# Four small TensorE items queued at other places of a two-block transformer kernel

## The reference

```
h = rmsnorm(x, g_mix);  z = h @ w_in
cb, cc, cv, q, k, v, f_logit, gate_c, gate_a = split(z)
log_f = log_sigmoid(f_logit + b_f)                 # one column per head, 8 heads
c = cumsum(log_f over the tokens)
logits = q k^T / sqrt(128) + c[query] - c[key], causal; attn = softmax(logits) v
conv_y = cb * causal_dwconv(cc * cv)
x = x + (sigmoid(..) * (conv_y @ w_conv_out) + sigmoid(..) * (attn @ w_attn_out)) @ w_mix_out
x = x + square(relu(rmsnorm(x, g_mlp) @ w_ff1)) @ w_ff2
x = rmsnorm(x, g_final)
```

## Time and profile before

| | |
|---|---|
| median of three runs | 2388.35 us |
| the three runs | 2388.16, 2388.35, 2389.65 us |
| profiled execution | 2390.3 us, of which the span of its instructions is 2388.2 us |
| PE busy | 2378.5 us of the span (100% in the page's rounding) |
| PEld, DVE, ACT busy | 2035.8, 1700.8, 1216.2 us |
| weights and the rest moved | 452.14 MB, mean 189 GB/s |

### The profile page before, as it was taken

One profiled execution on the slowest core, in us unless ns is written; L12 is line 12 of the kernel. 1 busy time (PEld: TensorE's weight loads), 2 busy tenths in 40 slices (PEclk: granted clock), 3 DMA queues, 4 the chain that ended last, 5 costly groups with the idle time before them and its releaser, 6 DMA issues.

```text
span 2388.2 us, 30674 instructions
## 1 busy us (share of the span) xinstructions
PE 2378.5 (100%) x12581; PEld 2035.8 (85%) x12581; DVE 1700.8 (71%) x1804; ACT 1216.2 (51%) x1427; POOL 0.2 (0%) x4
## 2 busy tenths in 40 slices
PE   9999999999999999999999999999999999999999
PEld 8788888888888888888888888888888888888887
DVE  5565666666567868868868667855788777886788
ACT  5354454555544545445445555555555455545554
POOL 0000000000000000000000000000000000000000
PEclk9999999999999999999999999999999999999999
DMA  7557566665565675656665565555655665566655
GB/s 252 160 162 204 161 196 192 192 188 197 189 185 172 216 223 183 218 175 203 200 192 188 183 185 168 168 177 185 186 181 193 199 193 177 183 217 189 187 171 181
DMA packets 238040, 452.14 MB, mean 189 GB/s; under 512 B 16570, under 2 KB 20780, under 8 KB 237772
## 3 DMA queue, kind: packets, MB, share of 16 engines
q1 hardware_dynamic: 237147, 449.07, 59.4%
q10 hardware_dynamic: 752, 1.12, 0.1%
HBM read 446.46 MB, written 3.67 MB: 188 GB/s over the span
## 4 chain that ended last, share of the span: by engine, by line
PE 96%; DVE 3%; ACT 1%; DMA 0%; issue 0%; SPq 0%; DVEq 0%; ACTq 0%
PE PS L72 96%; DVE WL L72 1%; ACT WH L72 1%; DVE PB L72 0%; DVE PT L72 0%; DVE XT L72 0%; DMA RAW<-in_w_in 0%; DVE TB L72 0%; DVE TA L72 0%; ACT TA L72 0%; ACT SQ L72 0%; DVE XHL L72 0%; ACT TB L72 0%; DVE TC L72 0%; DVE SEL L72 0%
## 5 line engine op out<-in xcount | busy, mean ns | idle before, releaser
L72 DVE TENSOR_TENSOR WL<-RAW,WH 128x1024 fp32r<-128x1024 f32 (+1 forms) x844 | 1001.8, 1204 | 517.0 <-ACT WH L72 514.9
L72 PE MATMUL PS<-XHL,WH 128*128 128x512 f32 x3984 | 1254.1, 396 | 2.2 <-DVE CR L72 1.3
L72 ACT ACTIVATE WH<-RAW 128x1024 fp32r<-128x1024 f32 (+1 forms) x845 | 867.1, 1041 | 735.7 <-PE PS L72 721.4
L72 PEld LDWEIGHTS PS<-XHL,WL 128*128 128x128 f32 x3968 | 746.1, 188 | 176.3
L72 PE MATMUL PS<-XHL,WL 128*128 128x256 f32 x3968 | 780.3, 278 | 0.0
L72 PE MATMUL PS<-WH,MHL 128*128 128x512 f32 x2000 | 624.6, 390 | 0.0
L72 PEld LDWEIGHTS PS<-XHL,WH 128*128 128x128 f32 x3984 | 607.2, 188 | 6.5 <-DVE CR L72 1.5
L72 PEld LDWEIGHTS PS<-WH,MHL 128*128 128x128 f32 x2000 | 375.5, 188 | 78.3 <-DVE XHL L72 0.4
L72 PE MATMUL PS<-WL,MHL 128*128 128x512 f32 x1000 | 389.1, 389 | 0.0
L72 PEld LDWEIGHTS PS<-WL,MHL 128*128 128x128 f32 x1000 | 187.8, 188 | 37.9
L72 ACT ACTIVATE MHL<-TA 128x1024 fp32r<-128x1024 f32 x33 | 35.0, 1061 | 121.9 <-DVE TA L72 121.9
(11 more groups left out here) (150 smaller groups left out, 1211.2 us busy)
## 6 DMA issues: line engine op xcount, KB each, us to landing
RAW<-in_w_ff SPq DMA_DIRECT2D x256, 512.0 KB, 4.1
RAW<-in_w_in SPq DMA_DIRECT2D x224, 512.0 KB, 3.9
RAW<-in_w_up SPq DMA_DIRECT2D x176, 512.0 KB, 4.1
RAW<-in_w_down SPq DMA_DIRECT2D x88, 512.0 KB, 4.4
RAW<-in_w_mix_out SPq DMA_DIRECT2D x32, 512.0 KB, 3.9
RAW<-in_w_out SPq DMA_DIRECT2D x32, 512.0 KB, 3.7
RAW<-in_w_conv_out SPq DMA_DIRECT2D x16, 512.0 KB, 3.7
RAW<-in_w_attn_out SPq DMA_DIRECT2D x16, 512.0 KB, 4.2
```

The lines of the kernel that those rows point to most:

```text
L72: ins = step[1](*step[2], **step[3])
```

## The change

Four numbers that place small items are altered. The work itself stays the same: no instruction is added or removed.

```
@@ folded: the generator that empties a projection
             v = fold(*it)
             yield
+            for _ in range(fresh):
+                yield
             if fresh:
-                yield
                 spread(key)
                 yield
...
-        later(proj_evac(it, "q0", Q1, 0, "r1", SCALE, fresh=True))
+        later(proj_evac(it, "q0", Q1, 0, "r1", SCALE, fresh=3))
...
-        it = token_item(stream(w1, 0, ALLK, C0["v"], 512, 2), XHL, xtok, 512, {4: [log_f_item], 7: [running_item]})
+        it = token_item(stream(w1, 0, ALLK, C0["v"], 512, 2), XHL, xtok, 512, {4: [log_f_item]})
...
-        m = attention1(0, 6)
-        it = w1_item("cc", 0, m[0])
+        m = attention1(0, 5)
+        it = w1_item("cc", 0, {1: [running_item], **m[0]})
...
-            mid = ({4: [lambda: turn_x_item(0, G_AT2, nxt)], 6: [lambda: turn_x_item(1, G_AT2, nxt)]} if g == 2 else
-                   {5: [lambda: turn_x_item(2, G_AT2, nxt)]})
+            mid = ({4: [lambda: turn_x_item(0, G_AT2, nxt)]} if g == 2 else
+                   {1: [lambda: turn_x_item(1, G_AT2, nxt)], 5: [lambda: turn_x_item(2, G_AT2, nxt)]})
```

## The result

| | before | after |
|---|---|---|
| median of 18 executions | 2389.76 us | 2384.20 us |
| lowest, highest | 2388.16, 2390.59 | 2383.82, 2387.82 |
| mean of the 18 | 2389.36 | 2384.71 |
| profiled execution, its span | 2390.3, 2388.2 | 2383.82, 2382.0 |

The ratio is 0.998, with a 95% interval from 0.9974 to 0.9987: the changed kernel is faster by 0.13 to 0.26%. The forecast was 2383.9 us.

A forecast was written before the change was run, and what follows sets the result against it. PE was taken to bound the kernel, busy 2378.5 of 2388.2 us. Waits of 1.2 + 1.5 + 0.65 + 1.15 = 4.5 us off a fall-free median of 2388.35 gave 2383.9 us, with its own range 2383.1 to 2384.7.

The forecast's parts named there:

- Spread: Spread in k's projection, one unit later: PE's wait for TA, which VectorE finishes, goes; 1.2 us.
- Running sums: Sums moved from before cc to behind its unit 1: the wait for CR ahead of cc's first weights goes; 1.5 us.
- Q and K: Their products one unit earlier in cc: cv's wait for PB and its slow first step go; 0.65 us.
- Transposes: Second quarter's, moved into group 3: 0.88 us lost to the split and 0.28 at group 3's start go; 1.15 us.
- covers that were costed at nothing: Later RB and Q, XT due 1.8 us after it is ready, and XHL among weight splits: no new waits.
- The fall of the clock: At the running sums, clock at 0.50 over four steps of cc; should go, another 1.5 us in executions that have it.
- the median run of before has none: Before's median of 2388.35 us taken as free of the clock's fall; the rival, that it has it, 2382.3 us, chance 0.2.
- Several high runs of before: Sign that the forecast is wrong: several executions of before stand high, where two of three timed ones stood low.

The follow-up runs named there:

- the transposes alone: Before with only the second quarter's transposes moved into group 3; 9 of 11 executions between 2387.02 and 2387.79 us (middle 2387.19).
- the filled kernel: Before with six dense float32r products behind the running sums, where PE otherwise idles; five executions at 2388.40 to 2388.70 us, six at 2389.76 to 2390.23.
- the spread alone: Before with only the spread one unit later; 8 of 11 executions between 2386.87 and 2387.29 us (middle 2387.09).
- the products alone: Before with only the products of Q and K of the first four heads one unit earlier; 7 of 11 between 2387.47 and 2388.11 us (middle 2387.84).
- six zeros: The changed kernel with six instead of eight products of zeros ahead of the first transpose; median 2385.11 us.
- the sums alone: Before with only the running sums moved behind unit 1 of cc; 10 of 11 executions between 2387.02 and 2387.43 us (middle 2387.11).

## Why the prediction was right, and where not

The price of each wait, read from start times, held. Spread: 1.2 forecast, 1.27 by the traces, 1.34 by times alone. Running sums: 1.5 forecast, 1.3 measured; I had taken the whole idle time of the loads, of which 0.19 us stays even when nothing is waited for. Q and K: 0.65 forecast, 0.6 measured. Transposes: 1.15 forecast, 1.24 measured. The sum of 4.5 us is 4.35 to 4.6 between lower groups. All covers that were costed at nothing held as well: no wait for V, XT or a further WL appears.

The fall of the clock was priced right where it occurs (1.5 us, and the two traces differ by the 5.9 us that contain it), and it goes with the sums. In the kernels that have the sums at their old place with the idle wait behind them, 26 of 114 executions with a record of the clock have a mean of 0.999: 20 of 81 of before, two of 11 each with the spread, the products or the transposes alone. In those that have the sums inside cc, 0 of 74. With the wait filled, 0 of 11, where some 2 or 3 were to be expected. That the fall goes with the sums at their old place is thus shown by the counts. That it is the idleness behind them, and not the place as such, rests on the filled kernel alone and is likely rather than shown: at the rate of the 114, 11 executions without a fall come up by chance about once in 17 times, and once in 10 at the rate of before on that chip (4 of 21). That the clock falls in only some executions is shown by the profiles (a granted clock of 0.57 from 88 to 92 us with the spread alone, of 1.00 with the products alone). It agrees with what the prediction took from the Trainium skill, "TensorE: Matmul & The Clock Gate", section "Part 1: The HAM clock gate"; that a freely running window is the reason isn't tested by it.

The step that failed is the one I had called a choice: "the median run of before has none", and with it the reading that the upper group of before is the fall. Several high runs of before were one of the prediction's own signs of being wrong, and they came. The executions of before above 2389.3 us are 39 of 81, and only 20 of these carry the mark of the fall. The others have it from elsewhere, and at 18 executions the median of before lay in the upper group, at 2389.76 instead of 2388.35. The slow start is the cause that profiles show, but only in the changed kernel and in the filled one; whether it makes all 19 unmarked slow executions of before stays open, since no trace of one of these was taken. The records show one thing more that I had not looked for: the fall and the second cause never come together in before. They cost 1.5 and about 1.4 us, so both together would stand near 2391.3, and the highest of all 99 executions of before is 2390.78; if the two were independent, some six of the 20 marked ones should be that high. What ties them together isn't known. I had also expected the changed kernel to have a single group, and it kept a third of its executions 1.4 us high, from the start of the kernel, which no part of the change touches. The two errors lie on the two sides of the difference: 2384.20 against a forecast of 2383.9, but 5.56 us less than before by medians where I had said 4.5. By means it is 4.65. That the time came out within 0.3 us is partly luck: the forecast was counted from a low median of before, and the changed kernel's own median is low only because two thirds of its executions start quickly. With six zeros, where most start slowly, the median was 2385.11.

## What to carry to other kernels

A small item that borrows the buffer of the next big one belongs inside a projection, a unit or two away from its end, not at the end: then its result is taken out under cover, and what was a wait on both sides costs only its own matmuls. Price such a wait by the start times before and behind it against the same passage without a wait, not by the idle time in the list, which showed 3.4 us for what was worth 4.5 (0.28 us of it at the start of group 3, where the list of PE shows no wait). And where a few microseconds matter, look at all single times before taking a median, since two groups can move it by more than the change does.

## What was not expected of the hardware

- The clock at the start. In three profiles of upper executions (2385.39 and 2385.19 us of the changed kernel, 2389.76 of the filled one) the first two groups of four transposes took 0.95 to 1.12 us each instead of 0.6 to 0.66, and q came 1.1 to 1.5 us later, while the granted clock read 1.00. In every profile with eight zeros ahead the first products ran at half speed: 3.8 us for eight of them, where four take 1.06 at full speed. Where only the first group was that long (the spread alone, the sums alone), q was not late. Two more products of zeros brought the share of such executions down, two fewer brought it up.
- The same weak stretch, 2.8 us with 1.5 of them idle, let the clock fall to 0.50 for 3.4 us in some executions (profiles of before and of the spread alone) and not in others (profiles of the products and of the transposes alone).
